# The even layer's mixer on Trainium2: where VectorE divides the attention weights and where it cuts the weights' low parts

## The reference

```python
def mixer_attn_rglru(h, w_in, q_g, k_g, conv_w, conv_b, ga_w, ga_b, gx_w, gx_b, lam, w_out):
    proj = h @ w_in                                     # 1024 -> 2560
    q, k, v, xr, gate = jnp.split(proj, ...)            # 512 each
    q = rms_norm(q by head, q_g); k = rms_norm(k by head, k_g)      # 4 heads of 128
    # three dilated windows, each: s = q k / sqrt(C), masked; p = exp(s - m); o = p v / sum(p)
    # joined over the windows by a softmax of their log sums
    xc = conv_b + sum(xpad[:, j:j + S] * conv_w[j] for j in range(4))
    r = sigmoid(xc @ ga_w + ga_b); i = sigmoid(xc @ gx_w + gx_b)    # 4 blocks of 128
    log_a = -8 * r * softplus(-lam); a = exp(log_a)
    u = sqrt(-expm1(2 * log_a)) * (i * xc)
    hs = scan(a, u)                                     # hs[t] = a[t] * hs[t-1] + u[t]
    y_b = hs * gelu(gate)
    return concatenate([o_a, y_b]) @ w_out
```

## Time and profile before

| what | value |
|---|---|
| median of 3 executions | 1762.71 us (1761.33 to 1763.09) |
| the profiled execution | 1759.92 us, its span 1758.6 us |
| mean granted TensorE clock | 0.989 |
| busy: TensorE, VectorE, ScalarE, GpSimd | 96%, 70%, 51%, 10% |
| HBM read | 288.46 MB, 165 GB/s over the span |

### The profile page before, as it was taken

The page is one execution under the profiler, slowest core; times in us unless marked ns, Lnnn a source line. Parts: engine busy times, 40 slices in busy tenths (PEclk is TensorE's granted clock), DMA queues, the critical chain, the costliest instruction groups (busy, mean ns, idle before and its releaser), DMA issues.

```text
span 1758.6 us, 24398 instructions
## 1 busy us (share of the span) xinstructions
PE 1688.6 (96%) x10133; PEld 1490.4 (85%) x10136; DVE 1233.5 (70%) x1487; ACT 892.5 (51%) x1149; POOL 184.6 (10%) x166
## 2 busy tenths in 40 slices
PE   7979999999999999999999899999999999899997
PEld 6768998888999888888889688888888898688886
DVE  7865667765656777677767758778787667677764
ACT  6544455544545545455544545555555445455542
POOL 0500110011101001100021001003200111010002
PEclk9999999999999999999999899999999999999999
DMA  7333335555433555555554214555555543135551
GB/s 280 138 124 140 127 137 193 192 192 195 167 141 136 195 211 184 192 181 183 201 181 158 91 49 181 183 189 215 178 190 190 194 178 120 48 144 180 185 200 60
DMA packets 41439, 291.09 MB, mean 166 GB/s; under 512 B 4720, under 2 KB 4976, under 8 KB 7024
## 3 DMA queue, kind: packets, MB, share of 16 engines
q1 hardware_dynamic: 39456, 282.61, 44.6%
q10 hardware_dynamic: 1872, 6.92, 1.0%
HBM read 288.46 MB, written 1.05 MB: 165 GB/s over the span
## 4 chain that ended last, share of the span: by engine, by line
PE 82%; DVE 11%; ACT 4%; issue 2%; POOL 1%; DMA 0%; ACTq 0%; DVEq 0%; POOLq 0%
PE ps L298 36%; PE ps L297 18%; PE ps L295 4%; DVE w_lo L1399 4%; PE ps L286 3%; PE ps L288 3%; PE ps L287 3%; PE ps L331 3%; PE ps L333 3%; PE ps L332 3%; PE ps L296 2%; DVE xT L1407 2%; ACT w_hi L888 1%; POOL stat L2054 1%; PE ps L437 1%
## 5 line engine op out<-in xcount | busy, mean ns | idle before, releaser
L1399 DVE TENSOR_TENSOR w_lo<-raw,w_hi 128x2048 fp32r<-128x2048 f32 x268 | 613.6, 2293 | 232.1 <-ACT w_hi L888 228.2
L298 PE MATMUL ps<-xT,w_hi 128*128 128x512 f32 x1736 | 619.7, 396 | 0.0
L888 ACT ACTIVATE w_hi<-raw 128x2048 fp32r<-128x2048 f32 x268 | 510.1, 1904 | 215.1 <-PE ps L298 117.7
L297 PE MATMUL ps<-xT,w_lo 128*128 128x256 f32 x1736 | 485.0, 279 | 0.0
L298 PE MATMUL ps<-hT,w_hi 128*128 128x512 f32 x1168 | 412.5, 397 | 0.0
L298 PEld LDWEIGHTS ps<-xT,w_hi 128*128 128x128 f32 x1736 | 326.4, 188 | 67.4
L297 PEld LDWEIGHTS ps<-xT,w_lo 128*128 128x128 f32 x1736 | 327.9, 189 | 11.5
L297 PE MATMUL ps<-hT,w_lo 128*128 128x256 f32 x1168 | 327.1, 280 | 1.7 <-DVE hT L1584 1.7
L298 PEld LDWEIGHTS ps<-hT,w_hi 128*128 128x128 f32 x1168 | 219.3, 188 | 50.9
L297 PEld LDWEIGHTS ps<-hT,w_lo 128*128 128x128 f32 x1168 | 220.3, 189 | 5.0 <-DVE hT L1584 2.9
L940 ACT ACTIVATE tmp<-ps 128x512 f32<-128x512 f32 x120 | 71.7, 598 | 257.6 <-PE ps L298 257.6
(11 more groups left out here) (254 smaller groups left out, 2068.7 us busy)
## 6 DMA issues: line engine op xcount, KB each, us to landing
raw<-weights_dram SPq DMA_DIRECT2D x264, 1024.0 KB, 4.8
raw<-weights_dram SPq DMA_DIRECT2D x4, 768.0 KB, 4.1
tmp<-mem_dram ACTq DMA_DIRECT2D x2, 1024.0 KB, 7.0
x<-x_in_dram SPq DMA_DIRECT2D x2, 512.0 KB, 5.6
raw<-weights_dram SPq DMA_DIRECT2D x2, 512.0 KB, 6.5
arena<-mem_dram ACTq DMA_DIRECT2D x1, 1024.0 KB, 7.9
arena<-pool_mat_dram ACTq DMA_DIRECT2D x1, 1024.0 KB, 4.8
tmp<-masks_dram ACTq DMA_DIRECT2D x1, 768.0 KB, 8.3
```

The costliest lines, as they stand in the source:

```text
L297: pe.matmul(ps[:, bank, 0:S], lo, src[:, k, 0, :], start=False, stop=False)
L298: return pe.matmul(ps[:, bank, :].rearrange("p (a n) -> p a n", a=2), hi, src[:, k, :, :], start=False, stop=last)
L888: act.activation(b.w_hi[:, s, 0:w], b.raw[:, s, 0:w], ACT.Copy).then_inc(*mark("hi", u))
L1399: dve.tensor_tensor(b.w_lo[:, s, 0:w], b.raw[:, s, 0:w], b.w_hi[:, s, 0:w].bitcast(F32), ALU.subtract).then_inc(*mark("lo", u))
```

## The change

Only the order within the lists of VectorE and ScalarE changes; no instruction is added or taken away, and the lists of TensorE, GpSimd and SyncE stay as they are.

- VectorE cuts unit 6's low part before the memory's mean and the small steps of the decay rate, and unit 7's before the mean and the gate's polynomial; the mean comes behind both. ScalarE rounds unit 7 directly behind unit 6.
- Unit 11's low part comes behind the reciprocals, before the three last steps of the decay.
- The heads 0, 1 and 2 are divided earlier: head 0 before the memory's key rows and unit 14's low part, head 1 before unit 15's low part and the scan's input, head 2 before unit 16's low part and the scan.

```diff
@@ ScalarE's list
     highs(6)
+    highs(7)
     act.wait_ge(*at("lam", "abs"))
     act.activation(b.rg[:, 2, :], b.rg[:, 1, :], ACT.Exp, scale=-1.0).then_inc(*mark("lam_exp"))
     gate, gtmp = b.arena[:, 8, :], b.arena[:, 9, :]
     act.wait_ge(*at("scaled", "gate", 1))
     act.activation(gtmp, gate, ACT.Square).then_inc(*mark("gate_sq"))
-    highs(7)
     act.wait_ge(*at("gate_arg"))
@@ VectorE's list
     halves_sum(gate4[:, 2:4, :], hid15, 2, "sum", "gate", 1)
-    memory_mean("mem1", 2)
+    lows(6)
...
     for j in range(2):
         scaled(gate4[:, 2 * j:2 * j + 2, :], "gate", j, "x0")
-    lows(6)
+    lows(7)
+    memory_mean("mem1", 2)
...
     dve.tensor_tensor(zz, zz, ee, ALU.mult).then_inc(*mark("lam", "z"))
-    lows(7)
     for ch in range(1, 4):
         even_conv(ch)
...
         dve.reciprocal(dec[:, 512 * j:512 * j + 512], dec[:, 512 * j:512 * j + 512]).then_inc(*mark("decay", 1 + j))
+    lows(11)
     dve.wait_ge(*at("decay", 2))
...
     dve.scalar_tensor_tensor(r, aa, 1.0, r, ALU.add, ALU.mult).then_inc(*mark("decay_sq"))
-    lows(11)
     dve.wait_ge(*at("qgain", 0))
...
     lows(13)
     largest("at0", 0, 4)
     largest("at0", 1, 5)
+    normalized("at0", 0, True)
     key_rows(0, 0, (0, 1))
     lows(14)
-    normalized("at0", 0, True)
     largest("at0", 2, 4)
+    normalized("at0", 1, True)
     lows(15)
     dve.wait_ge(*at("decay_root"))
     dve.wait_ge(*at("input_gate"))
     dve.tensor_tensor(ig, ig, r, ALU.mult).then_inc(*mark("scan_in"))
-    normalized("at0", 1, True)
     largest("at0", 3, 5)
+    normalized("at0", 2, True)
     lows(16)
     dve.wait_ge(*at("scan_in"))
     for ch in range(4):
         s_ = dve.tensor_tensor_scan(...)
     s_.then_inc(*mark("scan"))
-    normalized("at0", 2, True)
     dve.wait_ge(*at("scan"))
```

## The result

The changed kernel took 1741.99 us (median of 4 executions, 1740.08 to 1746.45), the one before 1762.02 us beside it: ratio 0.9887, 95% interval 0.9874 to 0.9900, thus 17.6 to 22.2 us less. The forecast was 1743.3 us, a ratio of 0.989. The profiled execution took 1742.12 us, its span is 1740.8 us, 17.8 less than before.

The account below looks back on a forecast made before the run. TensorE bounds the kernel, losing time only in mixer waits (15.1 us) and slow-clock stretches behind them (7.2). Waits 12.1 plus stretches up to 7.2, taken as 19.4, off 1762.7 give 1743.3 us; range 1740.5 to 1750, own 1741.5 to 1745.

Parts of the forecast that it names:

- Units 6 and 7: Mixer start: no wait before unit 6, gate products at 60.9 instead of 67.32; gain up to unit 8 5.9 us.
- The polynomial and the small product: VectorE before the convolutions: polynomial 3.7 us earlier, small product still ending with GpSimd's, last convolution at 58.9.
- Unit 11's low part was not held: Port shared with GpSimd: input gate's product ends 0.9 us before the reciprocals; a hold would cost up to 2.4 us.
- Unit 11 and the heads: Unit 11 at 83.4 without a wait; head transposes at 98.7, 107.2, 115.3, 122.7, the fourth 19.5 us earlier.
- the 7.2: Loss to low clock in the stretches behind four mixer waits, summed to 7.2 us and taken for an upper end.
- Behind 142.19 nothing is moved.: After the fourth head's transposes: no list changes, so the gain carries on; projection's start 19.4 us earlier.
- my own last test: Prediction is wrong if the difference at the projection is not the difference at the end.
- A: Low clock remains behind new waits of 1.7 and 0.6 us; with the port's hold 1745 to 1747 us; chance 0.18.
- B: Only the weight order helps, heads stay bound by something hidden behind the division; 1748 to 1752 us; chance 0.12.
- C: TensorE gains 19 us in the mixer but a later stage waiting for weights swallows it; 1762.7 us; chance 0.04.
- D: Slower: without the mixer's rests, TensorE gets less clock in long feed-forward stretches; 1773 us at 60 us slow; chance 0.04.
- the waits that were seen (15.1 us): Five TensorE waits in the even layer's mixer: 4.01, 2.88, 2.74, 2.01 and 3.49 us, together 15.1.

Follow-up runs that it names:

- e4: Kernel before with only unit 6's low part moved ahead of the memory's mean; ratio 0.9997 (0.9987 to 1.0008).
- f4: Changed kernel with unit 11's low part between the two halves of the reciprocals; 1743.73 us, ratio 0.9900 to the kernel before.
- e3: Kernel before with only the divisions of heads 0, 1 and 2 moved earlier; ratio 0.9953 (0.9939 to 0.9968).
- g1: Changed kernel with the divisions of heads 0, 1 and 2 back at their old places; ratio 0.9959 to the kernel before.
- f2: Changed kernel with the first turned keys' copies ahead of unit 19's rounding on ScalarE; 1741.73 us, ratio 0.9885 to the kernel before.
- f3: Changed kernel with low parts of units 8, 11, 13, fourth division and turned keys' copies also reordered against remaining waits; 1742.42 us, ratio 0.9886 to the kernel before.
- g3: The same kernel as f3, measured once more; 1744.31 us, ratio 0.9888 to the kernel before.
- e1: Kernel before with only the moves of units 6 and 7 ahead of the memory's mean; 1755.98 us, ratio 0.9965.

## Why the prediction was right, and where it was off

**Units 6 and 7.** Right to 0.1 us (60.94 for 60.9). e4 shows that the step's second half was needed: what is late next was unit 7, and without its move 4.0 us are worth 1.0.

**The polynomial and the small product.** The row of L1672 was read rightly as held by GpSimd, but I let it be held again. GpSimd's list has the memory's root ahead of the product, and since the mean moved next to the polynomial, the root delayed the product and the hold fell on the convolution: same length, 59.0 for 58.9 in the end. Unit 11's low part was not held, as forecast: the input gate's product ended at 80.57, 0.6 us before it (0.9 forecast), and it took 2.23 us. Moved to meet the product (f4), the low part still wasn't held, since it came first.

**Unit 11 and the heads.** Right; no step is off by more than 0.45 us. The largest error is the third transposes (115.3 for 114.87): from one head's transposes to the next TensorE took 8.2 and 7.8 us, where I had 8.5 and 8.1 from the old distances less their waits. A wait's row counts from a modelled end, and in an unbroken row (0.39 us long, 0.23 apart) the next matmul starts 0.16 before that end; so a wait that goes altogether frees about 0.2 more than it shows. This is an estimate from the rows; it also goes some way to explain why the 7.2 that I called an upper end for the slow stretches came out as 7.7. e3 and g1 give the divisions 10.9 and 10.7 us where the replay of e3 had 10.6.

**"Behind 142.19 nothing is moved."** True of the lists, not of the clock. In both profiles of the changed kernel the unchanged wait of 2.17 us is followed by a slow stretch that the profile of before did not have (e4 and g1 have it too), and of 19.65 us 18.75 were left at the projection and 17.8 at the end. That is the term the sum lacked, 1 to 2 us. By my own last test (the difference at the projection should be that at the end) the forecast failed by 0.95 us, and the projection came 18.75 earlier where I had 19.4. f2 shows the other side: with the wait at 0.74 the stretch is at 1.00.

**The rivals.** A, a low clock behind a wait that is left, came true in kind, but at a wait that I had not listed because the change doesn't touch it, and not behind the 1.71 and 0.80. In f4 it did come at the listed place, behind 1.96 us before the first transposes. B is out by e3, where the divisions alone bring 10.9 us. C is out by the total. D is out for the changed kernel, by both measurements of it; the small variant of it, a few us of low clock far behind, is open: f3 and g3 have it, and so have profiles with less of the change.

**Size.** 1742.0 and 1745.7 us against 1743.3: one session 1.3 below, the other 2.4 above and outside the forecast's own 1741.5 to 1745. That the first came so near is partly luck. Its profile gained 17.8 us over the span where 19.4 were forecast; the medians of that session differ by 20.0, those of the other by 16.8, and the nine executions of e3 alone lie up to 8.5 us apart. The positions up to the fourth transposes are no luck: they came out in both profiles.

## What to carry to other kernels

When an engine's list is fixed by hand, replay it from the trace's durations and ask at each removed wait what is late next: the waits that were seen (15.1 us) were worth 12 because three smaller ones took their place, and one of 4.0 us alone was worth 1. Put what the busiest engine waits for ahead of what nobody waits for yet, even at the price of a short wait for the exponentials. Judge each part beside the others as well as alone: all low parts without the divisions brought 9.0 us at the fourth transposes and the divisions alone 10.9, nearly the 19.65 of both, while unit 11's part was worth 2.0 alone and 2.9 beside the rest. A wait that grows behind a gain (2.74 to 4.57 us in g1) has not eaten it: compare positions, not waits.

## What the runs showed of the hardware

The loss behind a wait of TensorE is not fixed by the wait's length. After 2.91 us before unit 11 e4 ran at the full 2.4 GHz, after 3.11 us at the same place e1 ran five microseconds at 1.2 GHz, and f4 ran 3.5 us mostly at 1.2 GHz after 1.96 us before the first transposes. The wait of 2.17 us before the second transposes of keys had clock 1.00 behind it in six profiles and 0.64 to 0.66 in four. First e4, then f4:

```profile
91.50 0.50 PE L331 MATMUL ps<-w_hi,memT 128*128 128x512 f32 x1 [2.91 <-DVE w_lo L1399]
```

```profile
91.50:97.00 5.50, 5.50 (x24) 4.43 (x24) 5.50 (x4) 1.92 (x2) 0.00 (x0) 1.00 0.63 220
```

```profile
100.42 0.89 PE L429 MATMUL ps<-cst,arena 128*128 128x128 f32 x4 [1.96 <-DVE arena L1493]
```

```profile
100.40:103.90 3.50, 3.48 (x13) 2.94 (x14) 2.58 (x2) 0.60 (x1) 0.00 (x0) 0.54 0.27 37
```

The clock is 1.00 in the stretch of e4 and 0.54 in that of f4. The times follow the clock: nine executions of e3 fell into 1750.3 to 1752.3 us at a mean clock of 0.989 to 0.990 and 1758.6 to 1758.8 us at 0.985, the same kernel. The Trainium skill ("TensorE: Matmul & The Clock Gate", section "Part 1: The HAM clock gate") says that the number of slow matmuls of one kernel varies from run to run and that the penalty of the ramp is under one per cent of a typical kernel's span. The two groups here lie 0.4% apart. That is more than each of the smaller parts of this change, so these were read from the positions in the trace and not from the medians.
